# The down product of an MLP: from one plain product to seven products of quadrants, with weight sums made by adding DMAs

## What is computed

```
def sq_relu_mlp(h, w_up, w_down):
    return jnp.square(jax.nn.relu(h @ w_up)) @ w_down
...
        y = sq_relu_mlp(h, w_mlp_up[l], w_mlp_down[l])
        x = x + gt_f * rms_norm(y, g_post_mlp[l])
```

## Time and profile before

| what | us |
|---|---|
| median of 3 runs (lowest, highest) | 826.06 (825.58, 826.78) |
| span of the profiled execution, first to last instruction | 824.2 |
| median of the runs less this span | 1.9 |
| PE busy | 815.0 |
| DVE busy | 507.1 |
| ACT busy | 440.4 |
| POOL busy | 29.1 |
| down product, first matmul to end of the last | 644.7 to 818.8 |

### The profile page before, as it was taken

One profiled execution on the slowest core, in us unless ns is written; L12 is line 12 of the kernel. 1 busy time (PEld: TensorE's weight loads), 2 busy tenths in 40 slices (PEclk: granted clock), 3 DMA queues, 4 the chain that ended last, 5 costly groups with the idle time before them and its releaser, 6 DMA issues.

```text
span 824.2 us, 12511 instructions
## 1 busy us (share of the span) xinstructions
PE 815.0 (99%) x4292; PEld 704.3 (85%) x4292; DVE 507.1 (62%) x672; ACT 440.4 (53%) x655; POOL 29.1 (4%) x30
## 2 busy tenths in 40 slices
PE   8999999999999999999999999999999999999997
PEld 8887888888888888888888899999999888888885
DVE  4776666665585655665784688777776533333335
ACT  6557777776664443444243657666676632233332
POOL 1640000000000000000000000000000000000000
PEclk8999999999999999999999999999999999999999
DMA  9951433326096666676437031333333423322302
GB/s 320 348 159 33 118 109 108 107 78 182 26 271 190 201 188 178 193 204 178 128 127 231 1 103 52 103 102 102 103 109 119 155 103 102 99 82 99 102 1 102
DMA packets 132895, 109.52 MB, mean 133 GB/s; under 512 B 4460, under 2 KB 117252, under 8 KB 132868
## 3 DMA queue, kind: packets, MB, share of 16 engines
q1 hardware_dynamic: 132772, 109.12, 44.3%
q10 hardware_dynamic: 64, 0.02, 0.0%
q0 software_dynamic: 32, 0.02, 0.0%
HBM read 107.04 MB, written 2.10 MB: 132 GB/s over the span
## 4 chain that ended last, share of the span: by engine, by line
PE 94%; DVE 2%; ACT 1%; DMA 1%; issue 1%; SPq 0%; ACTq 0%; DVEq 0%
PE ps L438 31%; PE ps L439 30%; PE ps L440 30%; PE ps L1488 1%; DMA graw<-in_w_gate_i_dram 1%; PE ps L1509 0%; DMA erows<-in_b_mod_dram 0%; PE ps L1653 0%; PE ps L1496 0%; DVE sp L1075 0%; PE ps L1522 0%; DVE w_lo L1143 0%; PE ps L1625 0%; PE ps L1626 0%; PE ps L1535 0%
## 5 line engine op out<-in xcount | busy, mean ns | idle before, releaser
L438 PE MATMUL ps<-ht_hi,w_hi 128*128 128x512 f32 x448 | 175.5, 392 | 0.0
L439 PE MATMUL ps<-ht_lo,w_hi 128*128 128x512 f32 x448 | 174.7, 390 | 0.0
L440 PE MATMUL ps<-ht_hi,w_lo 128*128 128x512 f32 x448 | 174.4, 389 | 0.0
L1051 DVE TENSOR_TENSOR w_lo<-raw,w_hi 128x1024 fp32r<-128x1024 f32 x100 | 121.9, 1223 | 57.0 <-ACT w_hi L653 55.1
L653 ACT ACTIVATE w_hi<-raw 128x1024 fp32r<-128x1024 f32 x96 | 100.4, 1050 | 32.6 <-PE ps L440 30.9
L438 PEld LDWEIGHTS ps<-ht_hi,w_hi 128*128 128x128 f32 x448 | 84.3, 188 | 18.7 <-issue 1.0
L438 PE MATMUL ps<-w_hi,hd_hi 128*128 128x512 f32 x256 | 99.6, 389 | 0.0
L439 PE MATMUL ps<-w_lo,hd_hi 128*128 128x512 f32 x256 | 99.6, 389 | 0.0
L440 PE MATMUL ps<-w_hi,hd_lo 128*128 128x512 f32 x256 | 99.6, 389 | 0.0
L440 PEld LDWEIGHTS ps<-ht_hi,w_lo 128*128 128x128 f32 x448 | 84.3, 188 | 17.8
L439 PEld LDWEIGHTS ps<-ht_lo,w_hi 128*128 128x128 f32 x448 | 84.3, 188 | 17.1
(11 more groups left out here) (234 smaller groups left out, 1504.0 us busy)
## 6 DMA issues: line engine op xcount, KB each, us to landing
raw<-in_w_in_dram SPq DMA_DIRECT2D x48, 512.0 KB, 4.8
modraw<-in_w_mod_dram SPq DMA_DIRECT2D x32, 512.0 KB, 4.0
raw<-in_w_mlp_down_dram SPq DMA_DIRECT2D x32, 512.0 KB, 3.3
up_raw<-in_w_mlp_up_dram SPq DMA_DIRECT2D x56, 256.0 KB, 3.5
mod_raw<-in_w_mod_dram SPq DMA_DIRECT2D x32, 256.0 KB, 7.3
xs<-in_x_dram SPq DMA_DIRECT2D x8, 512.0 KB, 5.7
raw<-in_w_a_out_dram SPq DMA_DIRECT2D x8, 512.0 KB, 5.3
raw<-in_w_b_out_dram SPq DMA_DIRECT2D x8, 512.0 KB, 5.6
```

Of the source, the lines that this page charges most:

```text
L438: nc.tensor.matmul(dst, l_hi, r_hi, start=first, stop=False, skip_group_check=chained)
L439: nc.tensor.matmul(dst, l_hi, r_lo, start=False, stop=False, skip_group_check=chained)
L440: return nc.tensor.matmul(dst, l_lo, r_hi, start=False, stop=last, skip_group_check=chained)
L1051: V.tensor_tensor(w_lo[:, slot, :], raw[:, slot, :], f(w_hi[:, slot, :]), ALU.subtract).then_inc(w_lo_ready, 1)
```

## The change

The down product is written as seven products of quadrants too. The hidden activations are cut in four (features in two halves `upper`, tokens in two halves `late`), the weights in four (features in two halves, columns of D in two halves `right`). A product `D_A11 ... D_S4` has 16 feature blocks, 256 tokens (two blocks `tb`) and 512 columns: 16 x 2 x 3 = 96 matmuls, 672 in all, where there were 768. Work goes in 28 groups of four feature blocks; a group needs two weight chunks (128 partitions x 2 feature blocks x 512 columns, 512 KB each) and one split of activations, now 128 x 1024.

Four of the seven products need a sum of weight quadrants. S1, S2 and S4 use a running sum in a new buffer of eight chunks, `wsum`: SP loads one quadrant (`load_wsum`), and GpSimd's DMAs add the next onto it in SBUF (`accum_op=ALU.add`). S3's sum is made the same way in the `raw` slots and two extra ones (`raw_x`). That is 8 + 8 + 8 + 8 adding DMAs of 512 KB, at most four in flight. A11, A12, A22 and the base of S3 are 32 plain loads, `wsum` 8 more: 72 transfers where there were 32. The sums of activations are made by DVE in place (`hidden_sum`, 16 of 128 x 1024). Banks: two for each of three accumulators; between products ACT copies six results out and DVE adds six (`down_copy`, `down_add`), and PE waits for some of them (`DOWN_AFTER`). The loops over units become straight code.

```diff
+        D_A11, D_A12, D_S1, D_S2, D_S3, D_A22, D_S4 = range(PRODUCTS)
+        RAW_SLOT = {D_A11: (0, 1, 2, 3, 0, 1, 2, 3), D_A12: (0, 1, 2, 3, 0, 1, 2, 3),
+                    D_S3: (0, 1, 2, 3, RING, RING + 1, 0, 1), D_A22: (2, 3, 0, 1, 2, 3, 0, 1)}
+        ADDED = ([(D_S1, c) for c in range(CHUNKS)] + [(D_S2, c) for c in range(CHUNKS)]
+                 + [(D_S3, c) for c in range(RING + 2)] + [(D_S4, c) for c in range(CHUNKS)]
+                 + [(D_S3, c) for c in range(RING + 2, CHUNKS)])
...
+            def load_chunk(i, upper, right):
+                for c in same_slot(i)[-1:]:
+                    sp_eng.wait_ge(w_lo_ready, split_count(U_DOWN + c))
+                sp_eng.dma_start(down_raw[down_slot(i)].rearrange("p (k n) -> p k n", k=2),
+                                 w_dn_part(upper, right, i % CHUNKS)).then_inc(down_raw_in[down_slot(i)], 16)
...
+            def add_rows(n, dst, upper, right, c):
+                if n >= len(pool_in):
+                    wait_added(pool, n - len(pool_in))
+                pool.dma_start(dst.rearrange("p (k n) -> p k n", k=2), w_dn_part(upper, right, c),
+                               accum_op=ALU.add).then_inc(pool_in[n % len(pool_in)], 16)
+            for n, (p, c) in enumerate(ADDED):
+                if p == D_S1:
+                    pool.wait_ge(rows_in[c], rows_before(c) + 16)
+                    add_rows(n, wsum[:, WSUM_SLOT[c], :], 1, 1, c)
+                elif p == D_S2:
+                    pool.wait_ge(w_lo_ready, split_count(U_DOWN + CHUNKS * D_S1 + c))
+                    add_rows(n, wsum[:, WSUM_SLOT[c], :], 0, 0, c)
+                elif p == D_S4:
+                    pool.wait_ge(w_lo_ready, split_count(U_DOWN + CHUNKS * D_S2 + c))
+                    add_rows(n, wsum[:, WSUM_SLOT[c], :], 1, 0, c)
+                else:
+                    i = CHUNKS * D_S3 + c
+                    pool.wait_ge(down_raw_in[down_slot(i)], plain_count(i))
+                    add_rows(n, down_raw[down_slot(i)], 0, 1, c)
...
+            for a in range(2, DGROUPS * PRODUCTS):
+                hidden_hi(a)
+                down_hi(2 * a)
+                if a == DGROUPS * D_S3:
+                    down_copy(d_u2, D_S2, 0)
+                down_hi(2 * a + 1)
...
+            for a in range(DGROUPS * PRODUCTS):
+                p, g = divmod(a, DGROUPS)
+                pe.wait_ge(hd_lo_ready, a + 1)
+                for tb in range(2):
+                    if g == 0 and p in DOWN_AFTER:
+                        semaphore, count = DOWN_AFTER[p]
+                        pe.wait_ge(semaphore, count + tb)
...
```

More of the change, by code:

```diff
@@ L55, in hybrid_layer_kernel @@
     PRODUCTS, SPLITS = 7, 4
+    KHALF = FB // 2
+    GROUP = 4
+    DGROUPS = KHALF // GROUP
+    CHUNKS = 2 * DGROUPS
     w_in_v = w_in[0].rearrange("(k p) n -> p k n", p=P)
@@ new lines, in hybrid_layer_kernel, with rows_before, down_slot, same_slot @@
+        down_raw = [raw[:, j, :] for j in range(RING)] + [raw_x[:, 0, :], raw_x[:, 1, :]]
+        down_raw_in = raw_in + rows_in[CHUNKS:CHUNKS + 2]
+        def rows_before(b):
+            return 16 * len(range(b, NB * len(GROUPS), M0_BUFS))
+        def down_slot(i):
+            return RAW_SLOT[i // CHUNKS][i % CHUNKS]
+        def same_slot(i):
+            return [c for c in RAW_CHUNKS if c < i and down_slot(c) == down_slot(i)]
+        def plain_count(i):
+            slot = down_slot(i)
+            first = raw_count(U_DOWN) - 16 if slot < RING else rows_before(CHUNKS + slot - RING)
+            return first + 16 * len(same_slot(i)) + 16
@@ L1013, in _ @@
             over_pairs(act, pair)
-            down_hi(2, AFTER_P3)
-            hidden_hi(3, 3)
+            down_hi(2)
             hidden_f2_relu(NPAIR - 1, 1)
-            down_hi(3, AFTER_P4)
+            down_hi(3)
             hidden_f1(NPAIR - 1)
             hidden_f2(NPAIR - 1)
[L1021 to L1039, removed]
@@ L1440, in _ @@
             over_pairs(dve, pair)
[L1441 to L1453, removed]
+            split_lo_down(1)
@@ L1471, in _ @@
+            for t in range(2, TB):
+                down_add(d_u2, D_S4, t - 2)
+                dve.wait_ge(d_summed, summed_count(D_S4, t - 2))
+                z_gain(t, 0, d_u2[:, t - 2, :])
+                z_rows(t, t + 5)
         @block.tensor
@@ L1761, in _, with down @@
-            split_ready(0)
+            def down(a, tb, ks):
+                p, g = divmod(a, DGROUPS)
+                for k in ks:
+                    i = 2 * a + k // 2
+                    if k % 2 == 0:
+                        pe.wait_ge(w_lo_ready, split_count(U_DOWN + i))
+                    cs = slice(k % 2 * HALF, (k % 2 + 1) * HALF)
+                    mm = mm3(ps[:, D_BANK[p] + tb, :], hd_hi[:, a % 2, k, tb * P:(tb + 1) * P],
+                             hd_lo[:, a % 2, k, tb * P:(tb + 1) * P], w_hi[:, i % RING, cs], w_lo[:, i % RING, cs],
+                             p in (D_A11, D_A12, D_S1) and g + k == 0, g == DGROUPS - 1 and k == GROUP - 1, True)
+                return mm
@@ L1770, in _ @@
[L1770 to L1775, removed]
-            with pe.Fori(1, FB // RING - 1) as q:
-                for j in range(RING):
-                    split_ready(RING * q + j)
-                    for t in range(TB):
-                        mm = down(j, t, False, False)
-                    mm.then_inc(unit_done, 1)
```

333 lines of the change are left out of this document (243 added, 90 removed).

## The result

The changed kernel takes 843.23 us in the median (842.17 to 843.85), against 826.42 us for the kernel before on the same chip: a ratio of 1.0204, 95% interval 1.019 to 1.0219. It is about 2% slower, where 815 us and a range of 805 to 834 were forecast.

The account below looks back on a forecast made before the run. PE, busy for 99% of the span, was taken to bound the kernel: 826.06 - 21.8 (matmuls) + 0.7 (end) + 9.6 (waiting for transfers) = 814.6, say 815 us; own range 807 to 820, whole range 805 to 834.

Parts of the forecast that it names:

- The matmuls: Down stage on PE: 768 matmuls become 672 of the same shape, 96 x 0.2267 = 21.8 us less.
- ACT and DVE: Per group of 5.44 us, ACT needs 2.9 us and DVE 4.5; copies and adds between products are covered; nothing taken.
- The start: First group's double-width activation split would end on DVE at 644.6, where PE arrives at 644.72; nothing taken.
- what an add costs: An adding DMA of 512 KB on the engines: at least 1.35 us, twice the load 2.7; taken below 2.0 us.
- the first rival: An add costs two loads, 2.7 us: 22.4 us of waiting in all, 827.4 us, range 822 to 834; chance 0.30.
- the wait before S3's chunk 6: Sign of the double price: a second PE gap before S3's last group near 757, released by a `pool_in` wait.
- 9.6 us of gaps: PE waits early in the down stage for loads delayed by adds: chunk 4 first, 3 us, then chunk 5.
- how two queues share the engines: Adds and early loads share evenly, 9.6 us of waiting; bounds 0.6 if loads are undisturbed, above 18.5 at two thirds.
- the tail: After the last matmul, one DVE addition of 512 from PSUM goes ahead of the square: + 0.7 us.
- The double-price rival: An add takes 2.7 us, twice a plain load: 22.4 us of waiting, 827.4 us, range 822 to 834; chance 0.30.

Follow-up runs that it names:

- e1: Changed kernel with the 32 DMAs on GpSimd's queue loading plainly instead of adding, so its output differs; 821.62 us, 0.994 of the kernel before.
- e4: Changed kernel with the norm of token blocks 0 and 1 moved from behind the last product to between S4's groups; 840.02 us, ratio 1.0165.
- e2: Changed kernel with all eight adds of S3 ahead of S4's on GpSimd's queue; 836.95 us, ratio 1.0125.
- e5: Changed kernel with S3's adds before S4's, the first eight adds paced by PE's units, and the first two token blocks' norm moved up; 819.00 us, ratio 0.9908.
- e7: Changed kernel with 31, 41 and 51 filler matmuls on PE ahead of its waits for chunk 4, chunk 5 and S3's seventh chunk; 841.81 us, ratio 1.0184.
- e8: e6 with its first eight adds at units 4, 6, 7, 9, 11, 13, 15, 17; 812.79 us, ratio 0.9832.
- e6: e5 with A22's loads in six slots, chunks 4 to 9 ahead of `wsum` loads, and another pace of the adds; 812.10 us, ratio 0.9837.

## Why the prediction was wrong

**The matmuls** (21.8 us less): right. The distance stayed 0.227 us outside the stretches at the lower clock.

**ACT and DVE**, costed at nothing: right in the stage. No gap of PE was released by `hd_lo`, or by DVE being late of itself, even with DVE at 17.0 to 17.3 of 20 us in 690 to 730. The add and copy between products never showed.

**The start**: right, PE came at 644.72, 0.2 us later than before by the same view, and went on. The first add was issued at 644.13, where 645 was forecast.

**The step that failed: what an add costs.** "I take a price below 2.0 us, nearer to the plain load, the only measured one." It is 2.55 us, about twice the 1.33 of the same DMA without the add (e1). The prediction set aside what the Trainium skill's page "Collectives: The Full Stack", section "The bandwidth ceiling: the fold count and why AG ≠ RS ≠ AR", says of a reduction, that it sends two read descriptors for a chunk and runs at half the rate. The rate agrees here: 200 GB/s for adds alone against 385 for loads of the same packet size; descriptors are not to be seen in the trace.

With this price the first rival comes nearest: 43 us of loads and 32 x 2.55 = 81.6 us of adds are 125 us of transfers in 107 us, and the wait before S3's chunk 6 came where it was put (near 757 in the text, 768.8 in the trace, later by the longer wait at the start and the slow matmuls behind it). Its size does not follow from that sum, which gives 18 us of waiting in all where 28.1 were measured. The engines were not full throughout, as that sum takes them to be: from 685 to 705 us they were busy for 52 to 74%, while GpSimd's queue waited 37.6 us for DVE's split of S1's first chunk, and the other 24 adds began only at 707.47. What had to fit in time was those 24, 61 us at 2.55 us each, with the loads beside them.

With plain loads in place of adds the total comes out: 9.6 us of gaps were worked out, e1 has 9.7, and 814.6 plus terms that I had not seen, 3.8 us of clock, 3.4 of tail and 0.2 at the start, is 822.0 where e1 took 821.62. This is partly luck. The forecast had 3 us for chunk 4 and 6.6 for chunk 5; e1 has 7.1 and 2.7.

**The second failure: how two queues share the engines.** I let them share evenly and put two thirds for the adds as an upper bound, 18.5 us. In 653 to 665 us both moved as many packets, and an add's packet takes 1.8 times as long, so the loads got 39.4 against 70.3, about a third. The first two gaps are 16.5 us and not 9.6. That this wait is "the same for every price of an add from one to two loads" was wrong too: with plain DMAs (e1) it is 9.7 us, with adds 16.5, and all of the difference lies before chunk 5.

**The third, not in the sum at all: the clock.** I priced waiting as waiting only. Up to 7.0 us follow from it, most of them hidden as above.

**The fourth: the tail**, + 0.7 us for one addition. It was 4.1. I looked at what stands ahead of the last token block in its own chain and not at what is queued on DVE ahead of it: the norm of two other token blocks (5.5 us) and two gains (1.2), which before were spread between PE's last token blocks. e4 returned 3.0 of it.

The double-price rival said 827.4. With the measured terms put in it gives 827.4 + 5.7 (gaps of 28.1 and not 22.4) + 7.0 (clock) + 3.4 (tail) + 0.2 (start) = 843.7, measured 843.2; this is an account made afterwards and proves no term. The chances were off as well: that case deserved more than 0.30, and its range of 822 to 834 held no allowance for the clock or for shares other than half.

## What to carry to other kernels

A DMA that adds into SBUF cost the DMA engines about two plain loads here, and the loads beside it got a third of the engines; a plan that fits with plain loads must be summed up again with that weight, and its order chosen by when each sum is wanted, with single-use loads ahead. When work is taken off the bounding engine, sum up the transfers over each stretch between deadlines and not over the stage, since the average load (here 29% of the engines before) said nothing about them. And behind a last product look at the whole queue of each engine, not at the one chain: what was spread out before may now stand in a row.

## What was not expected of the hardware

- Two DMA queues moved as many packets (813 and 815 in 12 us) though the packets of one take 1.8 times as long; the slower kind set the rate of both, 131 GB/s each. In e1_plain the counts are equal too while both had work (280 and 279 packets from 652 to 656 us), though GpSimd's plain packets hold 4 KB and take longer than the loads' (66.0 against 37.5% of the engines). They part, 392 against 222 and 531 against 144 in the next two stretches of 4 us, where GpSimd's issues waited 3.2 and 5.0 us for landings.
- The issue of an adding DMA of 512 KB takes 1.20 us on GpSimd, a plain one 0.72, where 16 KB took 0.65. It is not what limits.
- PE idle for 6.9 us brought the granted clock to 0.50. It was still there through six matmuls and the next wait of 9.0 us, and 13 matmuls then ran 0.43 us apart before it rose again. Gaps of 2.3 to 2.5 us also left some matmuls behind them at the lower clock in e2, e5, e7 and e8, others as long did not: e6 has one of 2.4 us and a granted clock of 1.00 throughout.
